# A second mixer's attention with four dense products, their result thrown away, ahead of each unit's probability transposes

## The reference, cut to what matters

```python
y_a = mla_mixer(c_q, c_kv, k_rope, ...)          # 6 heads, causal
y_b = diff_mixer(dq, dk, dv, ...)                # 4 heads, each the difference of two softmaxes
y_c = swa_mixer(sq, sk, sv, sinks, ...)          # 6 heads, window of 128, bias and a sink
h = h + jnp.concatenate([y_a, y_b, y_c], axis=-1) @ w_out[l]
```

## Time and profile before

| | |
|---|---|
| time, median of 3 runs (lowest to highest) | 1356.95 us (1354.27 to 1357.89) |
| time of the profiled execution | 1353.27 us |
| its span, first to last instruction | 1351.1 us |
| TensorE busy, share of span | 97% |
| VectorE, ScalarE, GpSimd busy | 74%, 55%, 8% |
| mean granted TensorE clock, 1 being 2.4 GHz | 0.987 |
| the second mixer's attention loop | 1069.2 to 1129.1 us of the span |

### The profile page before, as it was taken

How to read it: one execution, slowest core, us unless ns; L and a number is a source line. 1 busy time by engine, 2 the same in 40 slices (tenths; PEclk the granted TensorE clock), 3 DMA queues, 4 the chain that set the end, 5 groups by cost and what they waited for, 6 DMA issues and landing times.

```text
span 1351.1 us, 24318 instructions
## 1 busy us (share of the span) xinstructions
PE 1306.3 (97%) x8479; PEld 1156.2 (86%) x8479; DVE 993.6 (74%) x1875; ACT 744.4 (55%) x1352; POOL 109.8 (8%) x171
## 2 busy tenths in 40 slices
PE   6989998889999999999999999999999999999997
PEld 6979998679999989999989899999998667988886
DVE  6778787767877778777776768777775455877775
ACT  5545555556555556555565566555554554555553
POOL 3330001110000000000011200000022110000000
PEclk9989999999999999999999999999999969999999
DMA  9998665525766656666659547666544202566660
GB/s 249 270 255 252 187 187 146 140 64 154 222 188 190 194 158 195 196 187 190 187 162 236 174 125 224 197 187 191 178 150 162 60 26 72 173 191 186 186 186 32
DMA packets 288988, 233.34 MB, mean 173 GB/s; under 512 B 8860, under 2 KB 263140, under 8 KB 288928
## 3 DMA queue, kind: packets, MB, share of 16 engines
q1 hardware_dynamic: 282272, 214.07, 53.5%
q0 software_dynamic: 6368, 18.37, 5.6%
q10 hardware_dynamic: 288, 0.10, 0.0%
HBM read 229.56 MB, written 7.55 MB: 175 GB/s over the span
## 4 chain that ended last, share of the span: by engine, by line
PE 87%; DVE 5%; ACT 4%; DMA 2%; issue 1%; POOL 0%; ACTq 0%; POOLq 0%; DVEq 0%; SPq 0%
PE gu L1834 41%; PE y L1846 16%; PE gu L2003 4%; PE y L1914 4%; PE gu L2095 3%; PE y L1880 3%; PE gu L1813 2%; DMA sb_w_raw<-in_ffn_w_gate 2%; PE y L2320 1%; PE y L1861 1%; DVE sb_w_lo L1175 1%; PE gu L2078 1%; PE gu L1861 1%; PE gu L2179 1%; PE y L2133 1%
## 5 line engine op out<-in xcount | busy, mean ns | idle before, releaser
L1834 PE MATMUL gu<-sb_act_t,sb_w_hi 128*128 128x512 f32 x1680 | 590.7, 396 | 0.0
L1175 DVE TENSOR_TENSOR sb_w_lo<-sb_w_raw,sb_w_hi 128x1024 fp32r<-128x1024 f32 (+1 forms) x406 | 494.4, 1222 | 109.1 <-ACT sb_w_hi L789 102.3
L789 ACT ACTIVATE sb_w_hi<-sb_w_raw 128x1024 fp32r<-128x1024 f32 (+1 forms) x406 | 424.5, 1052 | 86.1 <-PE y L1846 37.1
L1834 PE MATMUL gu<-sb_act_t,sb_w_lo 128*128 128x256 f32 x1680 | 436.3, 280 | 0.0
L1834 PEld LDWEIGHTS gu<-sb_act_t,sb_w_hi 128*128 128x128 f32 x1680 | 307.7, 188 | 56.5
L1834 PEld LDWEIGHTS gu<-sb_act_t,sb_w_lo 128*128 128x128 f32 x1680 | 316.9, 189 | 15.1
L1846 PE MATMUL y<-sb_hid_t,sb_w_hi 128*128 128x256 f32 x1216 | 215.0, 279 | 5.0 <-DVE sb_hid_t L1316 5.0
L848 ACT ACTIVATE sb_work<-gu 128x256 f32<-128x256 f32 x220 | 84.0, 383 | 240.1 <-PE gu L1834 232.5
L1846 PEld LDWEIGHTS y<-sb_hid_t,sb_w_hi 128*128 128x128 f32 x1216 | 191.1, 190 | 8.5 <-DVE sb_w_lo L1175 5.3
L1846 PE MATMUL y<-sb_hid_t,sb_w_lo 128*128 128x256 f32 x608 | 169.4, 279 | 0.0
L1295 DVE TENSOR_TENSOR sb_work<-gu,sb_work 128x256 f32<-128x256 f32 x220 | 92.7, 423 | 98.0 <-ACT sb_work L848 97.8
(11 more groups left out here) (306 smaller groups left out, 1651.5 us busy)
## 6 DMA issues: line engine op xcount, KB each, us to landing
sb_w_raw<-in_ffn_w_gate SPq DMA_DIRECT2D x88, 512.0 KB, 4.0
sb_w_raw<-in_ffn_w_up SPq DMA_DIRECT2D x88, 512.0 KB, 3.9
sb_w_raw<-in_ffn_w_down SPq DMA_DIRECT2D x88, 512.0 KB, 3.9
sb_w_raw<-in_odd_w_qkv SPq DMA_DIRECT2D x24, 512.0 KB, 5.1
sb_w_raw<-in_w_gate SPq DMA_DIRECT2D x22, 512.0 KB, 3.9
sb_w_raw<-in_w_up SPq DMA_DIRECT2D x22, 512.0 KB, 3.9
sb_w_raw<-in_w_down SPq DMA_DIRECT2D x22, 512.0 KB, 3.8
sb_w_raw<-in_even_w_in SPq DMA_DIRECT2D x12, 512.0 KB, 3.9
```

Of the source, the lines that this page charges most:

```text
L789: nc.scalar.activation(w_hi[:, slot, 0:w], w_raw[:, slot, 0:w], ACT.Copy).then_inc(hi_done, 1)
L1175: nc.vector.tensor_tensor(w_lo[:, slot, 0:w], w_raw[:, slot, 0:w], w_hi[:, slot, 0:w].bitcast(F32), ALU.subtract).then_inc(lo_done, 1)
L1834: ins = nc.tensor.matmul(gu[:, b, w, 0:width], part[:, s, cols], act_t[:, k, 0:width], start=(k == 0 and i == 0), stop=(k == KT - 1 and i ...
```

## The change

Units of the second mixer get four dense products ahead of their transposes. Each multiplies columns 0 to 127 of `meta_t` with columns 0 to 255 of it and writes 128 x 256 results into the half of bank 0 of `y` that the unit's transposes then overwrite. Nothing reads them. In the same edit the two waits change their order: the wait for the copy of the unit before comes first, then the products, then the wait for this unit's probabilities.

```diff
+            def fill_wait(un):
+
+                count = 4 if un.u >= SECOND_U[0].u else 0 if un.u < ODD_U[0].u else 0
+                for _ in range(count):
+                    nc.tensor.matmul(y[:, 0, 0:SEQ], meta_t[:, 0:P], meta_t[:, 0:SEQ], start=True, stop=True)
+
             def turn_probs(un):
-                pe.wait_ge(probs_ready, un.t + 1)
                 if un.t >= 1:
                     pe.wait_ge(probs_t_ready, un.t)
+                fill_wait(un)
+                pe.wait_ge(probs_ready, un.t + 1)
```

## The result

The changed kernel takes 1366.89 us (median of 20 runs, 1359.65 to 1378.79), the kernel before 1357.53 us in as many. The ratio is 1.0079, 95% interval 1.0058 to 1.0100 (it leaves a few disturbed executions out on both sides). I had forecast 1355.0 us and no change; the result is the second rival's, "the clock falls all the same, and the products are only added work", which was priced at 1365.5 us.

A forecast was written before the change was run, and what follows sets the result against it. TensorE was taken to bound the second mixer, with 20.5 us at 1.2 GHz. Products +7.4, pauses 0 and clock -9.4 gave -2.0 us, put on the median 1356.95: 1355.0 us, range 1349.8 to 1363.

The forecast's parts named there:

- second rival: Second mixer's loop: the clock falls all the same, products only add work; +8.5 us, 1365.5 us; chance 0.27, whole or part.
- Term 1: Second mixer's loop: 64 new products at 0.115 us each, all on the path, +7.4 us at full clock.
- Term 2: Ahead of the transposes: waits filled, -0.7 us, against added pauses, +0.7 us; sum 0, bounds -0.7 to +2.3.
- Term 3: Second mixer's loop: dense products hold the clock through the 20.5 us low stretch, -9.4 us; other bound 0.
- The median: Whole kernel: the -2.0 us put on the median of 1356.95, 3.7 us above the profiled execution, giving 1355.0 us.
- first rival: Second mixer's loop: products hold the clock, and timed executions lose more to it than the profiled one; 1351.3 us; chance 0.25.
- (1): Check in the loop: new products start 0.115 us apart at full clock, twice that at the low clock.
- (4): Check from fourth product to transposes: no more than 0.19 us, and no idle time put down to VectorE.
- (2): Check from the loop's first scores to last values: 59.9 us before, 57.9 with the clock held.
- (3): Check of granted clock in windows over the loop: 1.00 throughout.
- (5): Check at the start of the output projection: the clock's fall there, 3.5 us long, stays.

The follow-up runs named there:

- z1_early4: The change with only its 32 products ahead of the first swa unit, none from it on: 1362.87 us, ratio 1.0035 to the kernel before.
- x6_cover_only8: Kernel before plus eight dense products in each of the four first diff units, none ahead of the transposes: 1353.44 us, ratio 0.9983.
- x8_change_again: The changed kernel's same file run again for a second profile: 1366.62 us, ratio 1.0069 to the kernel before.
- x7_twelve_thin: The change with twelve thin products a unit (16 rows by 64 columns of weights) in place of four dense: 1423.58 us, ratio 1.0485 to before.
- x1_waits_only: The change without its products, only the two waits in changed order: 1363.87 us, ratio 1.0016 to the kernel before.
- x5_cover_only4: Kernel before plus four dense products in each of the four first diff units, none ahead of the transposes: 1366.74 us, ratio 1.0065.
- y1_burst: Kernel before plus 24 dense products at one place, ahead of the last diff unit's transposes: 1359.20 us, ratio 1.0005.
- y2_late12: Kernel before plus twelve dense products a unit from the first swa unit on, 96 in all: 1365.24 us, ratio 1.0036.
- y4_cover8_burst: Kernel before plus eight products in each first diff unit, twelve ahead of the transposes of the last diff and second swa units: 1355.23 us, ratio 0.9979.
- y3_early12: Kernel before plus twelve dense products a unit ahead of the first swa unit, 96 in all: 1358.25 us, ratio 0.9991.

## Why the prediction was wrong, by its own steps

*Term 1, the products, +7.4 us.* Right. The added work measured 7.1 and 7.2 us in two profiles by the loop, and 7.5 us between executions of equal clock. All of it lay on the path, as said.

*Term 2, pauses and waits, 0.* Right in sum. The two waits for VectorE are gone after: the product engine has none in the loop. A pause of 0.11 us stands between the fourth product and the transposes (0.57 us for four products at 0.115), a pause like those of before and within the bound given; in three units (1084.47, 1126.98 and 1130.45) it is 0.22 us.

*Term 3, the clock, -9.4 us.* This is the step that failed. Its price was right: kernels that hold the clock gain 0.0115 of mean clock, at 1.1 us for each 0.001 some 13 us, more than 9.4 since the mean execution loses more than the profiled one. What was wrong is "I take it that they hold the clock through the loop". I had argued from the odd mixer that dense products among small ones keep the clock up, while the rows gave 4.5 of them per us there (5.5 with the 60 of L2003 in that window) and 1.3 here; and I had counted them as spread over all units, though I had named the two stretches that have none. The runs show both to matter. With 44 or more products ahead of the swa units the mean clock is 0.987 to 0.992, with 32 or fewer 0.977 to 0.986, and the 32 from the swa units on did nothing that could be seen (z1_early4 against the change). The change has 32 ahead of them, 23.8 us of low clock in its profile and a mean clock of 0.980, that of the kernel before. They also stand in the units where they help less: of the executions with 32 in the first diff units (x6_cover_only8) six of 12 were at 0.990 or more, of those with the change's places (the change, x8_change_again and z1_early4) none of 42. Whether it is the place or the eight at a time is not told apart.

*The median.* I put the 3.7 us between the profiled execution and the median down to nothing in particular. They are the clock: the profiled execution was a fast one because its low stretches were short. The first rival had this half right (the timed executions do lose more to the clock) and the other half wrong.

*The second rival.* Right in kind, at 1365.5 us against 1366.89. Its remnant of low clock was not a remnant but the whole.

*The Trainium skill.* The page "TensorE: Matmul & The Clock Gate", Part 1, says that the clock is set by how busy the array has been. x7_twelve_thin bounds what "busy" may mean: an engine whose products fill 99% of the time (123.52 of 124.40 us) stayed at the low level. The table "Why this matters for your kernels" names idle gaps. They agree with the fall near the start, and with none of those in the loop.

*The checks.* (1) came out as forecast, and (4) but for the three pauses of 0.22 us; (2) and (3) came out as for the rival: 69.51 us to the output projection and a stretch at 0.50. (5) was wrong: the fall at the output projection is in neither profile of the changed kernel. Besides the kernel before, it is in those of x1_waits_only, x5_cover_only4, y1_burst, y2_late12 and y4_cover8_burst, some 3.4 us each, and in no other; what decides it stays open.

## What to carry to other kernels

Read the granted clock of every execution, not of one profile: here 1.1 us for each 0.001 of the mean explained nearly all of the spread, and comparing at equal clock gave the cost of added work to 1 or 2 us. Products that are thrown away can pay where a stretch of small products loses the clock, but here only when they were thick, enough, and ahead of where it falls; find that place first, for half of them in another place bought nothing. Count the added products in the trace and not in the edit. Work out what holding the clock could give (13 us here) before choosing how much to spend on it.

## What the runs showed of the hardware that was not expected

- With TensorE busy 123.52 of 124.40 us the clock stayed at 1.2 GHz, when the added products were 16 x 64; with 128 x 128 ones in the same places it was low for 6.8 us.
- Once fallen, the clock stayed low over small products for 20 to 44 us (before, x1_waits_only, x5_cover_only4, x6_cover_only8), though the same swa units ran at full clock where it had not fallen (y3_early12).
- Three low stretches of 24 to 38 us ended 2.7 to 3.0 us behind the first product of a run of 12 or 24 dense ones (y1_burst, y2_late12, y4_cover8_burst); runs of four did not end those of the change.
- The same program has low stretches of other lengths from one execution to the next: the kernel before ranges from 0.968 to 0.989 in mean clock. What starts a fall in one execution and not in another stays open, as does why 48 products in the first diff units held the clock in every execution and 32 there in only some.
